# Other dummy matmuls while the router decides: column tiles and narrower stationary blocks in place of six full ones

## The chip, the cores and the metric

The program runs on one core of one Trainium2 chip. The metric is the device time of one execution in microseconds, taken as the median of several executions. The core has the engines TensorE (PE; its weight loads are listed apart as PEld), VectorE (DVE), ScalarE (ACT), GpSimd (POOL) and SyncE (SP, which here issues the weight transfers).

## What is computed

A trunk of two layers on 256 tokens with 1024 features. Each layer normalises, projects, runs three token mixers side by side, projects back and adds; then comes a channel mixer, dense in layer 0 and a mixture of experts in layer 1. The part that matters is the start of the experts of layer 1:

```python
logits = jnp.einsum('bsd,de->bse', h, w_router).astype(jnp.float32)
top_val, top_idx = lax.top_k(logits, TOP_K)          # 2 of 8
top_w = jax.nn.softmax(top_val, axis=-1)
gates = jnp.sum(jax.nn.one_hot(top_idx, N_EXPERTS) * top_w[..., None], axis=-2)
for e in range(N_EXPERTS):
    out = out + gates[..., e:e + 1] * swiglu(h, w1[e], w3[e], w2[e])
```

## The kernel before

All weights stream through six slots. SP loads a block of 128 x 2048 fp32 values into a slot of `raw`; ACT rounds it to fp32r (`whi`, L505); DVE subtracts to get the remainder (`wlo`, L782). A product in full precision is three fp32r matmuls, high by high, high by low, low by high (`split3`, L1200 to L1202). The order of the work is written out by hand, one program for each engine, and semaphores join them: `lo_ready` counts remainders that are there, `block_used` counts blocks that PE has finished with. SP may load into a slot of `raw` when `lo_ready` says that its old block has been split.

Between the mixers of layer 1 and its experts stands the routing, a chain across PE and DVE:

1. PE turns the rows and computes the router's logits (128 x 8 results in bank 4), then signals `logit_ps`.
2. DVE picks the two best experts for each token in a run of small operations (`route`, L1011 to L1030), signals `chosen_sb`, and then computes `xn_lo`, the remainder of the normalised rows (L788, two operations on 128 x 1024).
3. While DVE decides, PE has nothing of the reference to do. It issues dummy matmuls, `keep_warm(6)`, whose result in bank 6 nobody reads. Each multiplies the identity by 256 columns of a table of constants, in fp32. The profile shows one fp32 matmul as two records of PE, each with its weight load.
4. PE waits for `chosen_sb` and sums up the places of the tokens in five small fp32 matmuls (L1628 to L1632), signals `place_ps`, and issues `keep_warm(2)`.
5. DVE waits for `place_ps`, computes places (L1037, L1038) and the selection matrix `pick` (L1004), then the gates (to L1056), then splits one more weight block (L782, block `MOE0+5`).
6. PE gathers the rows of the first expert (L1526, L1527), ACT and DVE split the result (`xe_hi`, `xe_lo`), and the loop over the eight experts begins. Each expert uses 42 blocks.

Two other places of the kernel matter for reading the trace. In the mixers, L1383 to L1385 multiply with 64 stationary columns and write to partitions 0 to 63 for even heads and 64 to 127 for odd ones: these are column tiles. A head issues L1383, L1384 and L1385 once each, and the heads follow one another in the program.

Of the kernel before, what the change touches and what calls it, by code (L numbers as in the profile page):

```python
# [26 lines left out]
P = 128  # L27
# [44 lines left out]
MOE0 = BASE[1] + N_MIX  # L72
CHUNKS = F_EXPERT // FC
PER_EXPERT = 6 * CHUNKS
SLOTS = 6
# [57 lines left out]
def trunk(nc, x_in, w_mix_in, w_mix_out, g_mix, rel_bias, gla_w_gate, gla_b_gate, gla_g_norm, conv_w,  # L133
# [4 lines left out]
    with ctx:  # L138
# [3 lines left out]
        def place(name, cols, dt=F32, offset=None):  # L142
            size = 1 if dt == U8 else 4
            where = at[0] if offset is None else offset
            t = nc.alloc_sbuf_tensor_at(name, [P, cols], dt, offset=where)
            if offset is None:
                at[0] += (cols * size + 31) // 32 * 32
            return t

        raw = [place(f"raw{i}", BLOCK) for i in range(RAW_FIXED)]  # L150
        whi = [place(f"whi{i}", BLOCK, F32R) for i in range(SLOTS)]
# [7 lines left out]
        consts = place("consts", K_COLS)  # L159
# [86 lines left out]
        bank = [ctx.enter_context(nc.psum_tensor(f"bank{i}", [P, 512], F32)) for i in range(8)]  # L246
        bias_dram = nc.dram_tensor("bias_by_distance", [P, NH * 512], F32).ap()

        def sem(name):
            return ctx.enter_context(nc.semaphore(name))  # L250

        raw_full = [sem(f"raw_full{i}") for i in range(SLOTS)]
        hi_ready, lo_ready, block_used = sem("hi_ready"), sem("lo_ready"), sem("block_used")
# [31 lines left out]
        def ident():  # L285
            return consts[:, K_ID:K_ID + P]
# [908 lines left out]
        def _(pe):  # L1195
            mm = nc.tensor.matmul
# [54 lines left out]
            def keep_warm(n):  # L1251

                for _ in range(n):
                    mm(bank[6][:, 0:256], ident(), consts[:, 0:256], start=True, stop=True)

            def bias_by_distance():

                pe.wait_ge(hot_loaded, 32)
                pe.wait_ge(rel_set, 2)
                for i in range(NH):  # L1260
                    mm(bank[(0, 1, 2, 7)[i]][:], setup_wide[0:REL_BUCKETS + 1, i * P:(i + 1) * P],
                       setup_hot[0:REL_BUCKETS + 1, :], start=True, stop=True).then_inc(bias_ps, 1)
# [4 lines left out]
            def mixer(l):  # L1267
                b = BASE[l]
                for t in range(NT):
                    if l and t:  # L1270
                        turn_rows(2, t)
                    pe.wait_ge(hT_ready, 8 * l + 2 * t + 2)
                    if l == 0 and t == 1:
                        bias_by_distance()
                    by_token([(b, 8)], 256, t, 5, 256 * t, None)
                    by_token([(b + 1, 4), (b + 2, 4)], 512, t, (4, 6)[t], 0, gr_ps)
# [345 lines left out]
                    ins = split3(bank[4][:, 8 * t:8 * t + 8], f_h, f_l, router_hi[:, 8 * k:8 * k + 8],  # L1622
                                 router_lo[:, 8 * k:8 * k + 8], k == 0, k == KD - 1)
            ins.then_inc(logit_ps, 1)
            keep_warm(6)
            pe.wait_ge(chosen_sb, 1)
            until = lev(LEVELS + 1)
            mm(bank[5][:, 0:8], until, chosen[:, 0:8], start=True, stop=True)  # L1628
# [40 lines left out]
```

## Time and profile before

| | |
|---|---|
| time, median of 3 runs | 1566.18 us (1565.23 to 1568.86) |
| span of the profiled execution | 1565.7 us |
| time of the profiled execution beside its span | the page gives none of its own; the span is 0.5 us under the median |
| PE busy | 95% of the span |
| DVE, ACT busy | 73%, 58% |
| DMA | 274 GB/s over the span |

### The profile page before, as it was taken

The numbers are of one execution on the slowest core, as the hardware profiler recorded it, in microseconds if no ns is written. First come the engines' busy times: TensorE is split into PE (matmuls) and PEld (weight loads), VectorE is DVE, ScalarE is ACT, GpSimd is POOL, SyncE is SP. The second block draws the span as 40 slices with busy tenths as digits, with TensorE's granted clock in tenths as the row PEclk, the third lists the DMA queues.
The fourth block names the chain that finished last, engine by engine and source line by source line (L and its number), as shares of the span: only waits on it lengthen the run. The fifth ranks groups of instructions, "written<-read, shape, count | busy, mean of one in ns | idle before, by whom it ended". The sixth has DMA issues, their size and how long they took to land.

```text
span 1565.7 us, 19299 instructions
## 1 busy us (share of the span) xinstructions
PE 1487.7 (95%) x7398; PEld 1228.4 (78%) x7398; DVE 1142.0 (73%) x862; ACT 908.4 (58%) x753; POOL 21.0 (1%) x36
## 2 busy tenths in 40 slices
PE   6998999997988999999999999999999999999995
PEld 4977788886977788878878878887887887887884
DVE  5476644445575688698698789879869869887983
ACT  4543433334633577576677576666757657767662
POOL 1000000001000000000000000000000000000000
PEclk8999999999998899999999999999999999999998
DMA  7831754324614499799799979979979989997990
GB/s 233 306 108 62 251 212 161 134 94 159 241 55 172 158 359 371 273 369 384 271 356 392 365 270 390 370 276 373 372 273 373 378 304 334 391 358 272 391 345 29
DMA packets 183905, 429.96 MB, mean 275 GB/s; under 512 B 6955, under 2 KB 13259, under 8 KB 183729
## 3 DMA queue, kind: packets, MB, share of 16 engines
q1 hardware_dynamic: 182304, 423.99, 74.0%
q0 software_dynamic: 1552, 5.32, 1.0%
q8 instruction: 32, 0.52, 0.1%
q14 instruction: 17, 0.13, 0.0%
HBM read 427.18 MB, written 2.10 MB: 274 GB/s over the span
## 4 chain that ended last, share of the span: by engine, by line
PE 83%; DVE 7%; issue 5%; ACT 2%; DMA 1%; POOL 0%; DVEq 0%; SPq 0%; ACTq 0%; POOLq 0%
PE bank L1200 26%; PE bank L1202 25%; PE bank L1201 25%; DVE wlo L782 3%; PE bank L1455 2%; DVE x L1121 1%; ACT whi L505 1%; DMA raw<-in_w_mix_in 1%; PE bank L1349 1%; PE bank L1527 1%; PE bank L1526 1%; PE bank L1311 1%; DVE f_lo L788 0%; DVE h L795 0%; DVE qk_level L857 0%
## 5 line engine op out<-in xcount | busy, mean ns | idle before, releaser
L782 DVE TENSOR_TENSOR wlo<-raw,whi 128x2048 fp32r<-128x2048 f32 x403 | 897.8, 2276 | 146.0 <-ACT whi L505 142.6
L505 ACT CAST whi<-raw 128x2048 fp32r<-128x2048 f32 x403 | 746.5, 1903 | 115.8 <-PE bank L1202 76.6
L1200 PE MATMUL bank<-whi,xe_hi 128*128 128x512 f32 x896 | 359.8, 402 | 1.4 <-DVE xe_lo L788 1.4
L1201 PE MATMUL bank<-wlo,xe_hi 128*128 128x512 f32 x896 | 354.6, 396 | 0.0
L1202 PE MATMUL bank<-whi,xe_lo 128*128 128x512 f32 x896 | 354.6, 396 | 0.0
L1200 PE MATMUL bank<-whi,gT_hi 128*128 128x512 f32 x536 | 212.7, 397 | 13.1 <-DVE e_gT_lo L788 11.0
L1201 PE MATMUL bank<-wlo,gT_hi 128*128 128x512 f32 x536 | 211.8, 395 | 0.0
L1202 PEld LDWEIGHTS bank<-whi,xe_lo 128*128 128x128 f32 x896 | 168.7, 188 | 41.0
L1200 PEld LDWEIGHTS bank<-whi,xe_hi 128*128 128x128 f32 x896 | 168.8, 188 | 39.8 <-DVE xe_lo L788 1.7
L1201 PEld LDWEIGHTS bank<-wlo,xe_hi 128*128 128x128 f32 x896 | 168.8, 188 | 38.0
L1202 PE MATMUL bank<-whi,e_gT_lo 128*128 128x512 f32 x448 | 177.0, 395 | 0.0
L667 ACT CAST gT_hi<-bank 128x512 fp32r<-128x512 f32 x56 | 32.8, 586 | 215.6 <-PE bank L1455 215.6
L1200 PE MATMUL bank<-whi,f_hi 128*128 128x512 f32 (+1 forms) x352 | 137.4, 390 | 18.0 <-DVE wlo L782 9.4
L1202 PE MATMUL bank<-whi,f_lo 128*128 128x512 f32 (+1 forms) x352 | 134.5, 382 | 0.0
L1201 PE MATMUL bank<-wlo,f_hi 128*128 128x512 f32 (+1 forms) x352 | 134.2, 381 | 0.0
L1200 PEld LDWEIGHTS bank<-whi,gT_hi 128*128 128x128 f32 x536 | 100.6, 188 | 40.4 <-DVE wlo L782 12.2
L1201 PEld LDWEIGHTS bank<-wlo,gT_hi 128*128 128x128 f32 x536 | 100.6, 188 | 23.9
L788 DVE TENSOR_TENSOR e_gT_lo<-bank,gT_hi 128x512 fp32r<-128x512 f32 x56 | 38.6, 690 | 87.9 <-ACT gT_hi L667 87.9
L1202 PEld LDWEIGHTS bank<-whi,e_gT_lo 128*128 128x128 f32 x448 | 84.1, 188 | 20.4
L1200 PEld LDWEIGHTS bank<-whi,f_hi 128*128 128x128 f32 x352 | 69.7, 198 | 32.7 <-DVE wlo L782 7.6
L1202 PEld LDWEIGHTS bank<-whi,f_lo 128*128 128x128 f32 x352 | 69.4, 197 | 12.1
L1201 PEld LDWEIGHTS bank<-wlo,f_hi 128*128 128x128 f32 x352 | 69.9, 199 | 11.3
(192 smaller groups left out, 1206.3 us busy)
## 6 DMA issues: line engine op xcount, KB each, us to landing
raw<-in_moe_w SPq DMA_DIRECT2D x336, 1024.0 KB, 7.4
raw<-in_ffn_w SPq DMA_DIRECT2D x33, 1024.0 KB, 5.8
raw<-in_w_mix_in SPq DMA_DIRECT2D x22, 1024.0 KB, 7.2
raw<-in_w_mix_out SPq DMA_DIRECT2D x8, 1024.0 KB, 4.9
raw<-in_w_mix_in SPq DMA_DIRECT2D x4, 544.0 KB, 3.9
x<-in_x SPq DMA_DIRECT2D x2, 512.0 KB, 4.8
bias_by_distance<-setup_bias POOLq DMA_DIRECT2D x1, 1024.0 KB, 5.1
bias<-bias_by_distance POOLq DMA_DIRECT2D x2, 512.0 KB, 7.3
```

The lines of the kernel that those rows point to most:

```text
L505: nc.scalar.copy(whi[w][:, 0:size], raw[s][:, 0:size]).then_inc(hi_ready, 1)
L667: nc.scalar.copy(e_gT_hi[:], bank[turned(c)][:]).then_inc(e_gT_h, 1)
L782: nc.vector.tensor_tensor(wlo[w][:, 0:size], raw[s][:, 0:size], whi[w][:, 0:size].bitcast(F32), ALU.subtract).then_inc(lo_ready, 1)
L788: nc.vector.tensor_tensor(dst, src, hi.bitcast(F32), ALU.subtract).then_inc(sem_out, 1)
L1121: nxt = nc.vector.scalar_tensor_tensor(x[:, o:o + 512], bank[(6, 4)[t] + j][:], gates[:, ds(turn + (e + EXPERTS * t), 1)], x[:, o:o + 512] ...
L1200: mm(dst, a_hi, b_hi, start=start, stop=False)
L1201: mm(dst, a_hi, b_lo, start=False, stop=False)
L1202: return mm(dst, a_lo, b_hi, start=False, stop=stop)
L1311: ins = mm(bank[(4, 7)[i % 2]][:, pr * SEQ + t * P:pr * SEQ + (t + 1) * P], log_a[:, t * 256 + pr * P:t * 256 + (pr + 1) * P], m, start=Tr ...
L1349: ins = mm(bank[5 + odd][:, g * P:(g + 1) * P], k[off:off + HD, o + t * P:o + (t + 1) * P], q[off:off + HD, o + tq * P:o + (tq + 1) * P], ...
L1455: ins = pe.transpose(bank[bk][:, q * P:(q + 1) * P], src[:, q * P:(q + 1) * P], ident())
L1526: mm(o, xn_hi[:, a:a + P], pick[:, t * P:(t + 1) * P], start=t == 0, stop=False)
```

## The change

The six dummy matmuls give way to 104. `keep_warm_in_tiles(rounds, width)` issues four fp32 matmuls in a round, each with 32 stationary columns of the identity and `width` moving columns, whose results lie in partitions 0 to 31, 32 to 63, 64 to 95 and 96 to 127 of bank 6. `keep_warm_with_weights(n, columns)` issues `n` fp32r matmuls with 512 moving columns of the first expert's first weight block and 128, 96 or 64 stationary columns, into bank 7; ahead of them stands a wait for that block's remainder. `keep_warm(2)` stays.

```diff
+            def keep_warm_in_tiles(rounds, width):
+
+                for _ in range(rounds):
+                    for g in range(4):
+                        mm(bank[6][32 * g:32 * (g + 1), 0:width], consts[:, 32 * g:32 * (g + 1)],
+                           consts[:, P + 256 * g:P + 256 * g + width], start=True, stop=True)
+
+            def keep_warm_with_weights(n, columns):
+
+                pe.wait_ge(lo_ready, MOE0 + 1)
+                w = whi[MOE0 % SLOTS]
+                for _ in range(n):
+                    mm(bank[7][0:columns, :], w[:, 0:columns], w[:, 512:1024], start=True, stop=True)
+
...
             ins.then_inc(logit_ps, 1)
-            keep_warm(6)
+            keep_warm_in_tiles(8, 256)
+            keep_warm_in_tiles(4, 512)
+            keep_warm_in_tiles(8, 128)
+            for columns in (128, 96, 64):
+                keep_warm_with_weights(8, columns)
             pe.wait_ge(chosen_sb, 1)
             until = lev(LEVELS + 1)
```

The order of PE's instructions between the logits (`router_hi`) and the gather (`xn_hi`), before; a row gives the line, output and inputs, the shape and the number of them:

```order
L1202 MATMUL bank<-router_hi,f_lo 128x8
L1254 MATMUL bank<-consts 128x256 x6
L1628 MATMUL bank<-small,consts 128x8 [waits chosen_sb]
L1629 MATMUL bank<-small,ones 128x8
L1630 MATMUL bank<-small,consts 128x8
L1631 MATMUL bank<-small,ones 128x8
L1632 MATMUL bank<-small,ones 128x8
L1254 MATMUL bank<-consts 128x256 x2
L1526 MATMUL bank<-pick,xn_hi 128x128 [waits pick_sb,xn_ready]
```

The same place now (`whi_53` is the slot of the first expert's first block; L1646 is what was L1628, L1540 what was L1526):

```order
L1202 MATMUL bank<-router_hi,f_lo 128x8
L1260 MATMUL bank<-consts 32x256 x32
L1260 MATMUL bank<-consts 32x512 x16
L1260 MATMUL bank<-consts 32x128 x32
L1268 MATMUL bank<-whi_53 128x512 [waits lo_ready]
L1268 MATMUL bank<-whi_53 128x512 x7
L1268 MATMUL bank<-whi_53 96x512 [waits lo_ready]
L1268 MATMUL bank<-whi_53 96x512 x7
L1268 MATMUL bank<-whi_53 64x512 [waits lo_ready]
L1268 MATMUL bank<-whi_53 64x512 x7
L1646 MATMUL bank<-small,consts 128x8 [waits chosen_sb]
L1540 MATMUL bank<-pick,xn_hi 128x128 [waits pick_sb,xn_ready]
```

Only what stands between the logits and the sums of places differs. The order of instructions on DVE, ACT and SP is the same as before.

## Rows read from the trace of the kernel before

**Rows 1.** The page: PE's busy time, and the chain that ended last.
```profile
PE 1487.7 (95%) x7398; PEld 1228.4 (78%) x7398; DVE 1142.0 (73%) x862; ACT 908.4 (58%) x753; POOL 21.0 (1%) x36
PE 83%; DVE 7%; issue 5%; ACT 2%; DMA 1%; POOL 0%; DVEq 0%; SPq 0%; ACTq 0%; POOLq 0%
```
**Rows 2.** Timeline of PE in the routing: start, length, operation, count [idle before].
```profile
514.31 4.34 PE L1254 MATMUL bank<-consts 128*128 128x256 f32 x12
518.49 0.28 PE L1628 MATMUL bank<-small,consts 128*128 128x8 f32 x2
...
519.30 0.37 PE L1632 MATMUL bank<-small,ones 128*128 128x8 f32 x2
...
521.19 0.30 PE L1526 MATMUL bank<-pick,xn_hi 128*128 128x128 f32 x1 [0.56 <-DVE pick L1004]
```
**Rows 3.** Timeline of DVE from the choice to the first expert.
```profile
517.79 0.17 DVE L1030 TENSOR_TENSOR small<-small 128x16 f32<-128x16 f32 x1
517.88 2.35 DVE L788 TENSOR_TENSOR xn_lo<-h,xn_hi 128x1024 fp32r<-128x1024 f32 x2
520.15 0.16 DVE L1037 TENSOR_TENSOR small<-small,bank 128x16 f32<-128x16 f32 x1
...
523.09 2.29 DVE L782 TENSOR_TENSOR wlo<-raw,whi 128x2048 fp32r<-128x2048 f32 x1
...
525.30 1.28 DVE L788 TENSOR_TENSOR xe_lo<-bank,xe_hi 128x512 fp32r<-128x512 f32 x2
```
**Rows 4.** Stretches, PE alone: bounds, length, busy (count), granted clock, DMA, GB/s.
```profile
514.24:517.40 3.16, 3.16 (x8) 0.51 0.95 382
517.40:521.16 3.76, 3.23 (x20) 1.00 0.59 228
521.16:524.90 3.74, 3.71 (x33) 1.00 0.00 0
524.90:526.60 1.70, 0.29 (x3) 1.00 0.16 16
527.90:531.00 3.10, 3.10 (x9) 0.50 0.64 245
```
**Rows 5.** Chain of waits at the first expert: start, length, what.
```profile
528.35 0.43 PE bank L1202
...
532.66 0.23 PE bank L1200
```
**Rows 6.** Timeline of PE: the last dummies of the first batch.
```profile
517.62 1.03 PE L1254 MATMUL bank<-consts 128*128 128x256 f32 x4
```
**Rows 7.** Timeline of PE: matmuls in 64-column tiles in the mixer of layer 1.
```profile
439.70 0.27 PE L1385 MATMUL bank<-pT,av 128*64 128x128 f32 x1
439.75 0.27 PE L1383 MATMUL bank<-pT,av 128*64 128x128 f32 x1
439.81 0.27 PE L1385 MATMUL bank<-pT,av 128*64 128x128 f32 x1
439.86 0.27 PE L1384 MATMUL bank<-pT,av 128*64 128x128 f32 x1
...
440.35 0.38 PE L1385 MATMUL bank<-pT,av 128*64 128x128 f32 x2
440.66 0.39 PE L1200 MATMUL bank<-f_hi,whi 128*128 128x256 f32 x1
```
**Rows 8.** Timeline of PE: fp32r, 512 moving columns, first and last of eleven.
```profile
490.52 0.39 PE L1200 MATMUL bank<-whi,f_hi 128*128 128x512 f32 x1
...
492.79 0.39 PE L1201 MATMUL bank<-wlo,f_hi 128*128 128x512 f32 x1
```
**Rows 9.** Waits of PE's two queues from 527 us on: total, times, longest.
```profile
PEld bank L1200 <- DVE wlo L782: 12.2, 6, 2.1
PE bank L1200 <- DVE e_gT_lo L788: 11.0, 7, 1.6
```
**Rows 10.** Waits of SP's transfers, 512 to 530 us: total, times, longest.
```profile
SPq L326 <- DVE wlo L782: 32.1, 3, 20.3
```

## The prediction

> **What bounds the kernel now.** I read the page first: PE is busy 95% of the span and holds 83% of the chain that ended last [rows 1]. Time added to PE's queue therefore counts unless it lies in a gap. So I went to the place of the change, in the timelines of PE and DVE. The reader is to see there who waits for whom. The first dummy starts at 514.31 us, and the first sum of places (L1628) starts at 518.49, its weight load right behind the last dummy [rows 2]. DVE's choice ends at 517.79 + 0.17 = 517.96 [rows 3], so the dummies already end a little after what they cover. The sums end at 519.30 + 0.37 = 519.67. But DVE reads them only at 520.15, since `xn_lo` holds it that long [rows 3]. PE thus has 0.48 us of slack, and no more: from L1037 on everything waits in a row, the gather at 521.19 on `pick`, the block's split at 523.09, `xe_lo` at 525.30, and the first expert behind it.
>
> Next the granted clock by stretches [rows 4]: 0.51 (1.2 GHz) under the first dummies, 1.00 (2.4 GHz) from 517.40, and 0.50 once more from 527.90 to 531.00, after a stretch from 524.90 in which PE was busy 0.29 of 1.70 us. In the chain of waits a matmul of the first expert takes 0.43 us in that low stretch and 0.23 us after it [rows 5].
>
> **What goes.** Six fp32 matmuls, 12 records, 514.31 to 518.49 less the sums' lag: in issue time 4.1 us. Eight records begin within the 3.16 us at the lower clock [rows 4]. At the higher clock four records run from 517.62 to the next matmul at 518.49 [rows 2, 6]: 0.87 / 4 = 0.217 us for 256 moving columns and half of an fp32 product.
>
> **What comes, in tiles.** The nearest rows are the 64-column tiles of the mixer [rows 7]. A record with 128 moving columns starts every 0.055 us while both tiles have work. In the last row, with one tile left, two records take 0.38 us, which is one duration of 0.27 and one pace of 0.11. So a record costs its tile 0.11 us for 128 columns, the same per column as the full-width dummies (0.217 for 256), and two tiles run side by side at full rate. I take this over to four tiles of 32. That was not in the trace, so it is the weakest step.
> - 8 rounds of width 256: 8 x 2 records x 0.217 = 3.5 us
> - 4 rounds of width 512: 4 x 2 x 0.434 = 3.5 us
> - 8 rounds of width 128: 8 x 2 x 0.109 = 1.7 us
>
> That is 8.7 us at the higher clock. If the tiles took turns it would be four times that, 34.7 us. Neither end can be excluded. I take the lower, as the one that the two-tile rows show. Below it I see no gain, since narrower stationary blocks did not shorten a record per moving column.
>
> One rule speaks against it. The rows show that tiles overtake one another: each head issues L1383, L1384 and L1385 twice each (two records), yet between two records of L1385 stands one of L1383, of the next head, and then L1384 mixes in at 439.86 [rows 7]. The Trainium skill, page "TensorE: Matmul & The Clock Gate", section "Part 3: Packing small matmuls — row/col tiling", says that matmuls start and end strictly in program order. By that rule the second record of a tile would hold back the next tile's first, and about two tiles at a time would run. The trace disagrees with it here, so its result stays a rival with a small chance. The same section gives 2.38x for three column tiles, which agrees with running side by side; no row here has three.
>
> **What comes, with weights.** 24 fp32r matmuls of 512 moving columns. Ten paces of such matmuls take 492.79 - 490.52 = 2.27 us [rows 8], so 24 x 0.227 = 5.4 us. For 96 and 64 stationary columns in fp32r there is no row. From below, 0.227 again (in rows 7 fewer stationary columns bought nothing). From above, the fp32 price of two records of 0.434, which makes 16 x (0.868 - 0.227) = 10.3 us more. I take the lower end, nearest in type. The added wait for `lo_ready` is free: it wants the expert's first block, and blocks are split in order, of which the sixth comes at 523.09 [rows 3] and the five before it ahead of the routing in DVE's program. If it were not free, the sums, and behind them DVE's L1037, would wait.
>
> Changes of the tiling cost a little: from the last L1385 (starts 440.35 + 0.11 = 440.46) to the next full-width matmul are 0.20 us, of which 0.11 is the record [rows 7]. Three changes at 0.1 make 0.3 us.
>
> **The clock.** 8.7 + 5.4 + 0.3 = 14.4 us of work at 2.4 GHz. The start lies where it lay, with the clock low until 517.40. Those 3.1 us do half the work, so 1.55 us is added: 16.0 us in all. The low stretch at the first expert may shift or vanish; it holds about eight matmuls at 0.43 instead of 0.23, so 1.6 us. The gap that comes before it stays as it is (it is DVE's split and `xe_lo`), so I keep the low stretch in the sum at its old price. If it vanishes, -1.6; if PE also gathers at 1.2 GHz, which it does for 3.74 us now [rows 4], up to +3.7.
>
> **The sum.** 16.0 - 4.1 = 11.9 us on PE, less the slack of 0.48: L1037 and all behind it move by 11.4 us. Does a later stage give it back? SP's queue has only three waits in this stretch, the longest 20.3 us, all for a slot that DVE has to split [rows 10], and the transfers stand still from 521.16 to 524.90 (0 GB/s) [rows 4]. So the weights are already as far ahead as six slots allow, and waiting longer loads nothing more, the block behind L782 excepted, which moves with L782. Nothing is given back. The ACT and DVE queues hold only work that needs PE. 1565.7 + 11.4 = 1577.1 us for an execution like the profiled one; the median lies 0.5 above that span, so 1577.6.
>
> **Rivals.**
> - *Two tiles at a time.* For: the rule above; four tiles were never seen. Against: rows 7 show overtaking. The tile part doubles, +8.7 us: 1586.3.
> - *Tiles take turns.* For: nothing in the trace but that four are unseen. Against: 0.055 against 0.11 us in rows 7. +26 us: 1603.6.
> - *The clock stays low through the tiles.* For: PE is said to be busy in rows 4 at either level, so being busy alone does not tell; each tile fills a quarter of the array. Against: four together fill it. Of 8.7 us of tiles, 7.1 us are then doubled beyond the 1.55 counted: 1584.7.
> - *Narrow fp32r costs as fp32.* +10.3 us: 1587.9.
> - *Not slower: the experts give the delay back.* PE's weight loads wait 12.2 us for `wlo`, in six waits of about 2 us [rows 9]. If blocks that come early filled these waits, 11.4 us of delay would be absorbed and the time would be about 1565.4. It decides from the point where the splits run a block further ahead. Against: the six waits are of one size and lie one to an expert, so they belong to the order of DVE's work at an expert's end, and all slots are full already.
>
> **How the numbers follow.** Chances: forecast 0.63, two at a time 0.12, turns 0.07, low clock 0.06, narrow fp32r 0.07, given back 0.05. The predicted time is the forecast's, 1577.6. Its own range is 1575.5 (the low stretch gone) to 1581.5 (gather at 1.2 GHz). The range for 8 in 10 takes in the three cases that end between 1584 and 1588 and leaves out the turns and the give-back: 1575.0 to 1588.5. What this kernel's measurement can tell from no change is about 0.2%, 3.1 us. All cases but the last lie above that: slower 0.94, within 0.2% 0.05, faster 0.01.
>
> **What would show each step.** In the timeline of PE, L1260 should have 64, 32 and 64 records; four of width 256 should start within 0.22 us at the higher clock. If one starts every 0.22, the tiles take turns; if two do, it is the rule of strict order. L1268 should have 24 records, one every 0.23 us, in all three widths; 48 would mean that fp32r fell back. The granted clock should rise at about 517.4. L1646 should start near 530.4 and DVE's L1037 should now wait for it, with no slack. PE's waits from the first expert on should be the same six and seven. The forecast is wrong if L1646 starts under 527 or over 533 us, or if the span grows by another amount than L1037 moves.

## The result, and the profile after

| | before | after |
|---|---|---|
| median of 3 runs | 1566.18 us | 1576.81 us (1575.81 to 1579.12) |
| span of the profiled execution | 1565.7 us | 1577.1 us |

The ratio is 1.0067, with a 95% interval of 1.0046 to 1.0087: slower by 0.7%. The forecast was 1577.6 us, and 11.4 us more for the profiled execution; the two profiled spans lie 11.4 us apart. The interval allows a growth of 7.2 to 13.6 us, so the times alone show the direction; the size is read from the stretches below.

Timeline of PE in the changed kernel, the columns as in [rows 2], the lines that answer to those rows:

```profile
514.43 10.13 PE L1260 MATMUL bank<-consts 128*32 128x256 f32 x160
524.49 5.80 PE L1268 MATMUL bank<-whi 128*128 128x512 f32 x24
530.13 0.28 PE L1646 MATMUL bank<-small,consts 128*128 128x8 f32 x2
...
532.38 0.30 PE L1540 MATMUL bank<-pick,xn_hi 128*128 128x128 f32 x1
...
537.82 0.79 PE L1200 MATMUL bank<-whi,xe_hi 128*128 128x512 f32 x1 [1.43 <-DVE xe_lo L788]
```

The dummies hold PE from 514.43 to 530.13, 15.7 us where it was 4.2. There are 160 records of tiles and 24 of fp32r. The gather starts 11.2 us later than in [rows 2].

Timeline of DVE, after, beside [rows 3]:

```profile
517.86 0.17 DVE L1030 TENSOR_TENSOR small<-small 128x16 f32<-128x16 f32 x1
517.95 2.35 DVE L788 TENSOR_TENSOR xn_lo<-h,xn_hi 128x1024 fp32r<-128x1024 f32 x2
531.34 0.17 DVE L1037 TENSOR_TENSOR small<-small,bank 128x16 f32<-128x16 f32 x1 [11.04 <-PE bank L1650]
...
534.28 2.29 DVE L782 TENSOR_TENSOR wlo<-raw,whi 128x2048 fp32r<-128x2048 f32 x1
...
536.49 1.28 DVE L788 TENSOR_TENSOR xe_lo<-bank,xe_hi 128x512 fp32r<-128x512 f32 x2
```

DVE is done with its choice at the same time as before and now stands for 11.04 us, released by PE's last sum. From L1037 on all steps keep their distances and have moved by 11.2 us.

Stretches of PE, after, with the columns of [rows 4]:

```profile
514.43:517.10 2.67, 2.67 (x29) 0.50 0.96 395
517.10:519.20 2.10, 2.10 (x44) 1.00 1.05 404
519.20:522.64 3.44, 3.44 (x36) 1.00 0.15 54
522.64:524.37 1.73, 1.73 (x68) 1.00 0.00 0
524.49:530.13 5.64, 5.64 (x29) 1.00 0.00 0
...
536.20:537.80 1.60, 0.19 (x2) 0.93 0.13 14
537.82:541.00 3.18, 3.18 (x8) 0.50 0.94 323
```

The fourth row is the one to read. It holds the 64 records of width 128 and the ends of the four before them: 1.73 / 64 = 0.027 us for a record, a quarter of the 0.109 that one costs its tile. The third holds the 32 records of width 512: 3.44 / 8 = 0.43 us for four side by side. The clock rises under the tiles, and it falls again at the first expert, as in [rows 4].

Chain of waits at the first expert, after (beside [rows 5]), and PE's waits from 538 us on (beside [rows 9]):

```profile
539.04 0.43 PE bank L1202
...
541.61 0.23 PE bank L1200
```
```profile
PEld bank L1200 <- DVE wlo L782: 12.2, 6, 2.1
PE bank L1200 <- DVE e_gT_lo L788: 11.1, 7, 1.6
```

PE's waits are what they were. From the first expert's first matmul to the end of the span are 1577.1 - 537.8 = 1039.3 us, and were 1565.7 - 526.6 = 1039.1.

### The profile page after: what moved, and what is told of

It is laid out like the page before. It is cut to its first block, busy times and chain, and to the rows that moved or that the text cites. A ratio compares the mean times of both kernels' runs of the same rounds, so it can differ in the third digit from the quotient of the medians.

```text
span 1577.1 us, 19643 instructions
## 1 busy us (share of the span) xinstructions
PE 1500.5 (95%) x7570; PEld 1236.8 (78%) x7570; DVE 1142.4 (72%) x862; ACT 908.7 (58%) x753; POOL 21.0 (1%) x36
## 4 chain that ended last, share of the span: by engine, by line
PE 84%; DVE 7%; issue 5%; ACT 2%; DMA 1%; POOL 0%; DVEq 0%; SPq 0%; ACTq 0%; POOLq 0%
PE bank L1200 26%; PE bank L1202 25%; PE bank L1201 25%; DVE wlo L782 2%; PE bank L1469 2%; DVE x L1121 1%; ACT whi L505 1%; DMA raw<-in_w_mix_in 1%; PE bank L1363 1%; PE bank L1541 1%; PE bank L1540 1%; PE bank L1325 1%; PE bank L1260 1%; DVE f_lo L788 0%; PE bank L1268 0%
## 5 line engine op out<-in xcount | busy, mean ns | idle before, releaser
L1200 PEld LDWEIGHTS bank<-whi,gT_hi 128*128 128x128 f32 x536 | 100.8, 188 | 40.3 <-DVE wlo L782 12.2
L1201 PEld LDWEIGHTS bank<-wlo,f_hi 128*128 128x128 f32 x352 | 69.6, 198 | 11.5
```

The source lines that it names most:

```text
L1200: mm(dst, a_hi, b_hi, start=start, stop=False)
L1201: mm(dst, a_hi, b_lo, start=False, stop=False)
```

## The experiments

Executions differ by some microseconds before the routing starts, and in how long after the first dummy the clock rises. So beside ratios I compare stretches within an execution. "Wall" runs from the first dummy to the first sum of places (without the six old dummies where these stay). "Work" is the wall less half of what lay at 1.2 GHz. Of the experiments, those for which no ratio is given were executed once, so their times are compared only roughly and their stretches carry the argument. A time is about 2.0 us above the span of its own execution; the expectations speak of spans.

| kernel | wall | at 1.2 GHz | work | first expert to the end | low stretch at the first expert |
|---|---|---|---|---|---|
| before | 4.2 | 3.1 | 2.6 | 1039.1 | yes |
| changed | 15.7 | 2.7 | 14.4 | 1039.3 | yes |
| plain_33 | 16.9 | 5.3 | 14.3 | 1038.6 | no |
| tiles_only | 11.2 | 5.0 | 8.7 | 1039.5 | yes |
| weights_only | 6.9 | 2.9 | 5.5 | 1037.8 | no |
| one_tile, tiles alone | 37.0 | 4.8 | 34.6 | 1037.6 | no |
| tile_by_tile, tiles alone | 26.3 | 6.0 | 23.3 | 1039.3 | yes |
| two_in_a_row, tiles alone | 11.3 | 5.1 | 8.8 | 1039.0 | yes |

### Is it only time on PE's queue?

```diff
 # plain_33, against the kernel before
-            keep_warm(6)
+            keep_warm(33)
```

> The kernel before with 33 full-width dummies in place of 6, chosen so that PE's queue gets as much time as in the changed kernel: 27 x 2 x 0.217 = 11.7 us more, so the sums of places start near 530.2 us. My theory (only the time that the dummies hold PE's queue counts, not their kind): span 1577.1 us within 0.5, as the changed kernel, and a ratio to before of about 1.007. Rival (tiles or fp32r blocks cost something of their own, by the array, by the clock or later on): the span differs from 1577.1 by more than 1 us though the sums start at the same time.

Measured: ratio to before 1.0083, interval 1.0056 to 1.0111, which overlaps that of the changed kernel. The span was 1575.9 us: 1.2 under the forecast, outside the band of the theory and just inside that of the rival. But in this execution the routing began 1.6 us earlier (the last logits at 512.51 and not 514.15 us, for reasons ahead of the change); from there to the end it took 1063.4 us, and the changed kernel 1063.0. The work is 14.3 us against 14.4; what differs is the clock, which rose 5.3 us after the first dummy and not 2.7, and did not fall at the first expert. So 66 full-width records and 184 records of the changed kernel cost the same, at the same work.

### The two parts alone

```diff
 # tiles_only, against the changed kernel
-            for columns in (128, 96, 64):
-                keep_warm_with_weights(8, columns)
 # weights_only, against the changed kernel
-            keep_warm_in_tiles(8, 256)
-            keep_warm_in_tiles(4, 512)
-            keep_warm_in_tiles(8, 128)
```

> The changed kernel without its 24 fp32r matmuls. Theory: the tiles hold PE for 10.1 us, as in the changed kernel, the sums start near 524.7 and not at 518.49, DVE had 0.48 us of slack, so the span is about 5.7 us over before, 1571.4. Rival (the clock, raised only by the full-width weights part, falls under tiles): low clock within the tiles and a span above 1573.

> The changed kernel without the tiles: 24 fp32r matmuls right behind the logits. Theory: 24 x 0.23 = 5.5 us, of which some 3 us of wall time at 1.2 GHz do half the work, 7.1 us in all; the sums start near 521.5, the span is 2.5 us over before, 1568.2. Together with the tiles alone (5.7) this falls short of 11.4 by what both pay or save once: the 4.2 us of old dummies and the slack. Rival (narrow fp32r blocks are slow when nothing warmed the array): L1268 paces above 0.25 at the higher clock, span above 1569.5.

Measured: tiles alone 1.0043 (1.0030 to 1.0056), weights alone 1.0023 (1.0008 to 1.0038). Expected were 5.7 and 2.5 us, which is 1.0036 and 1.0016; both lie in their intervals. The work of 8.7 and 5.5 us adds up to 14.2 of the changed kernel's 14.4; the rest is about what the changes of the tiling cost. In tiles alone the clock rose late, so its wall is 11.2 and not 10.1 us, but no low clock came back within the tiles. The groups of weights alone, by shape (busy, mean ns):

```profile
L1268 PE MATMUL bank<-whi 128*128 128x512 f32 x8 | 3.4, 599 | 0.0
L1268 PE MATMUL bank<-whi 128*96 128x512 f32 x8 | 2.0, 391 | 0.0
L1268 PE MATMUL bank<-whi 128*64 128x512 f32 x8 | 2.0, 392 | 0.0
```

Seven of the first eight lie in the low clock. 96 and 64 columns take the same time, in one record each: no fall-back to the fp32 price.

### Are four tiles really side by side, and does it need the order?

```diff
 # one_tile
-                        mm(bank[6][32 * g:32 * (g + 1), 0:width], consts[:, 32 * g:32 * (g + 1)],
+                        mm(bank[6][0:32, 0:width], consts[:, 32 * g:32 * (g + 1)],
 # tile_by_tile
-                for _ in range(rounds):
-                    for g in range(4):
+                for g in range(4):
+                    for _ in range(rounds):
```

> The changed kernel with all 80 narrow fp32 matmuls in the one tile of partitions 0 to 31; their number and shapes stay. Theory (four column tiles stream side by side, each at the full-width price per moving column): the tile part takes 34.7 us of work and not 8.7, so the span is 26 us over the changed kernel, about 1603. Rival (an fp32 matmul of 32 columns is simply a quarter of the price): 1577. Second rival (a quarter of the array in use does not raise the clock): paces of 0.43 for width 256 throughout, span near 1635.

> The changed kernel with the same matmuls ordered by tile: all of a width for tile 0, then for tile 1, and so on (16, 8 and 16 records of a tile in a row). Bounds for the tile part: 8.7 us of work if PE overtakes without limit, 34.7 us if it starts matmuls strictly in order, less an overlap of one record at each change of tile (33). The mixer's rows show overtaking across four records. I expect a window that reaches one tile ahead at least: 9 to 18 us, a span of 1577 to 1587. Rival (strict order): about 1601.

Measured: one tile 1603.12 us with a span of 1601.2 (expected about 1603), 34.6 us of work against 34.7. The same 160 records cost four times as much when they share a tile. Rows of its stretches of PE:

```profile
513.25:518.00 4.75, 4.75 (x13) 0.50 0.99 385
518.00:550.00 32.00, 32.00 (x149) 1.00 0.01 5
```

The clock rose with a quarter of the array's columns in use, so the second rival is out as well.

Tile by tile took 1593.93 us (span 1591.8) and 23.3 us of work, outside my 9 to 18: PE overtakes, but less far than I thought. Of a tile's 16 records of width 256, twelve start before the next tile's first, and the last four run beside it. Three stretches: one record at a time, two at a time, and then both (the counts take in records that are still in flight):

```profile
519.20:521.14 1.94, 1.94 (x13) 1.00 0.00 0
521.14:521.57 0.43, 0.43 (x5) 1.00 0.00 0
521.57:523.70 2.13, 2.13 (x14) 1.00 0.00 0
```

In the trace the four tiles' first records start at 512.98, 518.10, 521.14 and 523.76 us, and the next width's first at 526.38. At the higher clock that is every 2.62 us, 12 records of 0.217, not 16.

```diff
 # two_in_a_row, against the changed kernel
-                for _ in range(rounds):
-                    for g in range(4):
+                for _ in range(rounds // 2):
+                    for g in (0, 0, 1, 1, 2, 2, 3, 3):
```

> The changed kernel's narrow matmuls with two of a tile in a row (four records), then two of the next. From the tile-by-tile run, where a tile's first record always starts when the tile before it has three records waiting, I take the rule that PE may start a matmul past three waiting ones and not past four. Stepping through this order by that rule gives 10.0 us of work for the tile part (8.7 in the changed kernel, 23.0 tile by tile, by the same stepping). If it reached past only two, 13.7; strict order, about 26; two tiles at a time, 17.4. With about 1.5 to 3 us for the low clock, the tile part then holds PE for 11.5 to 13 us.

Measured: 1578.23 us (span 1576.2), 8.8 us of work with the 0.1 of the change behind it. The expected 10.0 was wrong, and so was my rule of three waiting matmuls, which had been fitted to one run. The first 16 records, all at 1.2 GHz:

```profile
512.51 1.96 PE L1260 MATMUL bank<-consts 128*32 128x256 f32 x16
```

The first four of them start at 512.510, .524, .537 and .550 us. The trace does not name a record's tile, but within one tile a record of this width starts only every 0.43 us at this clock, so these are one in each tile, though in the program the second, third and fourth tile's first are the fifth, ninth and thirteenth. Another picture fits everything seen here: each tile holds up to four records, and PE stops handing out when the next one's tile is full. Stepping through the orders by it gives 8.7 (changed), 8.7 (two in a row), 23.0 (tile by tile) and 34.7 (one tile). With three or five in place of four, tile by tile would take 25.9 or 20.1. In the mixer [rows 7] a head has six records, and the next head's first starts beside the third, when four are left. This picture was made after the last of these runs, and no run was made to test it alone.

### How cheap can such a matmul be?

```diff
 # width_32, against the kernel before; width_32_half has 16 rounds
             keep_warm(6)
+            keep_warm_in_tiles(32, 32)
```

> The kernel before with 32 rounds of four tiles with 32 moving columns behind the six dummies, 256 records of 32 stationary columns, all at the higher clock. If only the stream counts: 32 x 2 x 0.027 = 1.7 us more before the sums, span 1567.1. If the weight loads of the tiles take turns at a price that goes with their columns (0.055 for 64, as the pace of the mixer's tiles could also be read, so 0.027 for 32): 256 x 0.027 = 7.0 us, span 1572.3. If each record has a floor of 0.055: 14 us, span 1579.

> The 32-column matmuls of width 32 again, 128 records in place of 256. In the run with 256 PE issued 235 of them in 2.0 us, then stood still for 2.3 us with nothing to wait for but its own instructions, while a transfer on the instruction queue was under way. Theory (PE ate its instructions faster than they are fetched): no standstill here, 128 records in 1.1 us. Rival (a floor for each such matmul that shows up in lumps): about 1 us of standstill, 2.3 us in all.

Measured: a span of 1570.0 us with 32 rounds (1571.94 us of time), between the first two expected figures, and for a reason that none of them has. Timeline of PE:

```profile
514.42 0.59 PE L1254 MATMUL bank<-consts 128*128 128x256 f32 x1
514.94 2.18 PE L1260 MATMUL bank<-consts 128*32 128x32 f32 x235
519.26 0.39 PE L1260 MATMUL bank<-consts 128*32 128x32 f32 x21 [2.14 <-issue]
```

235 records start within 2.0 us, one every 8.4 ns. That is near the stream's 7 (0.027 for a tile, four tiles), and far under the 27 and 55 of the other two theories, which fall. Then PE stands still for 2.14 us with nothing to wait for. When it stops, one transfer has just begun on the instruction queue; this is the view of the queues for 516.8 to 518 us:

```profile
q8 instruction: 1, 0.02, 4.8%
```

The transfer takes 0.9 us, from 516.9 to 517.8, and PE starts again 1.4 us after its end. And the clock, which had risen, falls to 1.2 GHz for the whole gather (0.50 in 521.70 to 530.00), so the kernel pays far more than the standstill. With 16 rounds:

```profile
513.24 5.17 PE L1254 MATMUL bank<-consts 128*128 128x256 f32 x12
518.34 1.30 PE L1260 MATMUL bank<-consts 128*32 128x32 f32 x128
519.57 0.39 PE L1643 MATMUL bank<-small,consts 128*128 128x8 f32 x2
```

128 records without a standstill in 1.2 us, as expected, and 1568.13 us. That PE ran out of instructions fits both runs and the start of the transfer, but it is argued and not shown: what holds PE after the transfer stays open, and a cause that sets in only beyond 128 such records is not excluded.

### What the dummies are worth, and a version that might beat both

```diff
 # no_dummies, against the kernel before
-            keep_warm(6)
 # fill_gap, fill_gap_2 (the same), and after_fill_gap on the changed kernel
                 gather(EXPERTS * sweep)
                 turn_pick()
+                for _ in range(4):
+                    mm(bank[1][:, 0:256], ident(), consts[:, 0:256], start=True, stop=True)
```

> The kernel before without its first six dummies. Theory (the clock rises only where PE was dense before): PE idles from 514.4 to 518, the clock stays at 1.2 GHz, the gather of 3.7 us takes up to 7.2, and the span is 2 to 4 us over before, 1567.7 to 1569.7. Rival (the dummies do nothing for the time): 1565.7 within 0.5.

> The kernel before with four more full-width dummies behind the turned selection matrix, in the gap of 1.7 us ahead of the first expert, into a bank that the expert overwrites: 4 x 0.43 = 1.7 us. Theory (that gap is why the clock falls to 1.2 GHz at the first expert): no low stretch at 527.9 to 531.0, span 1.6 us under before, 1564.1; a ratio near 0.999, within the measurement's noise, so the spans decide. Rival (the half-dense gather alone makes it fall): the low stretch stays and the span is 1565.7 to 1565.9.

> The kernel before with the gap ahead of the first expert filled, a second look. The low stretch at the first expert was missing with the fill, but also without it in three other kernels (33 plain dummies, weights only, one tile) and present in four. Theory (the fill keeps it away): missing again. Rival (where the stretch between gather and expert falls against the clock's own steps decides): present about every second time.

> The changed kernel with the same fill. Theory (the fill keeps the clock up): no low stretch at the first expert, which in the changed kernel ran from 537.8 to 541.0; from the first expert's first matmul to the end 1037.6 us in place of 1039.3. Rival (where it falls against the clock's steps): the low stretch stays and that part takes 1039 or more.

Without the first dummies the ratio is 1.0031 (1.0015 to 1.0047), slower as expected, with a span of 1568.5 us. The stretches of PE show why:

```profile
512.70:516.70 4.00, 0.42 (x3) 0.50 0.93 366
516.70:520.30 3.60, 3.60 (x14) 0.50 0.40 153
520.30:527.30 7.00, 7.00 (x34) 0.50 0.27 73
```

PE idles, the clock does not rise, and the gather lasts some 7 us in place of 3.7. Six dummies of 4.2 us, nearly all of them under DVE's choice, are thus worth 2 to 7 us, and the 27 further ones of plain_33 cost their time. The loss does not come in each execution: three of the ten took 1564.3 to 1567.4 us, with a mean granted clock over the span of 0.982 to 0.984 where the other seven had 0.978 or 0.979.

With the gap filled the low stretch at the first expert was missing in all three profiled executions; without the fill it was there in six kernels of nine (not counting those two whose clock was low from earlier on). At three in nine it would be missing three times in a row by chance once in 27, so that the fill keeps it away is likely and not shown. Stretches of the changed kernel with the fill:

```profile
532.50:536.20 3.70, 3.67 (x33) 1.00 0.00 0
536.30:537.97 1.67, 1.67 (x10) 1.00 0.13 22
537.97:541.00 3.03, 3.03 (x15) 1.00 0.98 328
```

From the first expert to the end it took 1575.5 - 538.0 = 1037.5 us, as expected, and 1037.6 and 1037.5 in the two profiled executions of the kernel before with the fill: 1.6 us less than the 1039.1 with the low stretch. But the time of fill_gap against before is 1.0008 (0.9993 to 1.0023). A gain of 1.6 us is 0.1% and would come in only some of the executions, so it cannot be told from nothing by this measurement. No version is shown to beat the kernel before.

## Why the prediction was right

- *PE bounds, and the slack is 0.48 us.* Right. The sums start 11.64 us later and L1037 11.19, which makes the slack 0.45. DVE waits 11.04 us for PE's last sum, and nothing gives the time back.
- *Tiles, 8.7 us of work.* Right: 10.06 us from 514.43 to 524.49, of which 2.67 at half rate, leave 8.7. This was the step called the weakest, from two tiles to four. One tile alone needed 34.6.
- *The order of starts.* The rival of two tiles at a time would have made the tile part 17.4 us of work. It fell with the 8.7 us of the changed kernel, and again with two_in_a_row, where the fifth, ninth and thirteenth record of the program start within 0.04 us of the first. These traces thus disagree with the rule of the Trainium skill ("TensorE: Matmul & The Clock Gate", "Part 3: Packing small matmuls — row/col tiling") that matmuls start strictly in program order.
- *fp32r with weights, 5.4 us.* 5.64 us measured between the first and the sums: 0.230 a record and not 0.227, and the second record 0.1 late. Narrow blocks cost the same.
- *Changes of the tiling, 0.3 us.* About that much: 0.1 between tiles and weights, 0.1 at the second fp32r record, and 0.07 ahead of the first tile.
- *The clock.* It rose 2.7 us after the first dummy where I took 3.1, which made the wall 15.7 and not 16.0 us. This is chance: in fill_gap it took 6.1, which here would have made the wall 1.7 us longer. The low stretch at the first expert stayed, as kept in the sum; over other executions it comes and goes, and is worth about 1.6 us.
- *The sum.* 11.2 us at L1037 where 11.4 was forecast, 0.06 of them from ahead of the routing; that the span grew by 11.4 all the same is owed to 0.25 us more behind the first expert's start. That agreement to 0.1 us is partly luck. The median grew by 10.6, within what executions differ. The 0.5 us between median and profiled span was the distance of two executions: the profiled one after took 1579.12 us, the slowest of its three.
- *Slips in the working.* The case of delay given back takes off all 12.2 us of PE's waits and comes to 1565.4; less the 11.4 us of delay it is 1566.2. The ends of the forecast's own range follow as 1576.0 and 1581.3 from -1.6 and +3.7, not 1575.5 and 1581.5. Nothing else hangs on either.

Of the rivals, two at a time, turns, a low clock under tiles and the fp32 price each have a run against them. The experts gave nothing back: six waits of 12.2 us in all, as before.

## What to carry to other kernels

Work put on an engine that others wait for costs its time beyond the slack of the wait it hides in, in every shape tried here: what counts is how long it holds the engine. Read that slack as the difference between when a result is there and when its reader gets free (0.48 us here), not from busy shares. And dummies that keep the clock up paid here only as far as they fitted into such a wait: the first 4.2 us were worth some 5 us (2 to 7), the next 11.5 cost 11.2.

## What was not expected

- A burst of very short matmuls in four tiles stopped after 235 records (8.4 ns each), probably for want of instructions. PE stood for 2.14 us. Its clock fell 2.4 us after it had started again and stayed low for 13.6 us, from 521.7 to 535.3.
- How far PE reaches past a busy tile: four records of one tile is what fits three orders (tile by tile, two in a row, and the mixer's), found after the runs.
- 32 of 128 columns in use, one tile at a time, raised the clock as full-width matmuls did, and held it at 1.00 over the 32 us of the stretch shown.
- Between the first dummy and the rise of the clock lay 2.7 to 6.1 us in kernels alike up to there. Half of that spread, some 1.7 us, goes straight into the time and is a part of the scatter between executions.
